# The place of the convolution of the recurrence's input among VectorE's work of the input projection

## What is computed

```python
h = rms_norm(x, in_norm_g[l])
proj = h @ w_in[l]                       # 1024 x 10240
q, k, v, g, xr, gr, m_ret, m_rnn = jnp.split(proj, SPLIT_POINTS, axis=-1)
q = rotary(q...); k = rotary(k...) * (RET_QK_DIM ** -0.5)
xr = causal_depthwise_conv(xr, lru_conv_w[l], lru_conv_b[l])     # 4 taps along the tokens
hr = rg_lru(xr, ...)
y_rnn = (hr * jax.nn.gelu(gr)) @ w_rnn_o[l]
...
```

## Time and profile before

| | |
|---|---|
| median of 3 runs | 2019.1 us (2016.65 to 2019.78) |
| profiled execution | 2018.14 us |
| its span | 2016.4 us |
| busy: PE, PEld, DVE, ACT, POOL | 1984.3, 1655.6, 1381.0, 907.0, 231.4 us |
| mean granted clock of TensorE | 0.999 |
| passes of the convolution (L1955, L1958) | 8 and 24; the first starts at 88.7, the last at 216.9 us |

### The profile page before, as it was taken

How to read it: one execution, slowest core, us unless ns; L and a number is a source line. 1 busy time by engine, 2 the same in 40 slices (tenths; PEclk the granted TensorE clock), 3 DMA queues, 4 the chain that set the end, 5 groups by cost and what they waited for, 6 DMA issues and landing times.

```text
span 2016.4 us, 25123 instructions
## 1 busy us (share of the span) xinstructions
PE 1984.3 (98%) x9304; PEld 1655.6 (82%) x9304; DVE 1381.0 (68%) x1661; ACT 907.0 (45%) x1155; POOL 231.4 (11%) x188
## 2 busy tenths in 40 slices
PE   8999999999999999999999999999999999999998
PEld 6788888888888888887888888998788888888887
DVE  6876776776744444614876776847988788776766
ACT  6443353343445555412544543345644545543335
POOL 0000010010000000001254554300000000000000
PEclk9999999999999999999999999999999999999999
DMA  6343444445444443445333244731222122156533
GB/s 255 115 155 116 166 161 173 166 157 177 171 166 174 157 157 125 146 151 188 100 121 122 77 124 142 264 132 63 85 83 104 63 83 104 62 181 231 204 102 132
DMA packets 185636, 285.10 MB, mean 141 GB/s; under 512 B 9824, under 2 KB 123872, under 8 KB 185312
## 3 DMA queue, kind: packets, MB, share of 16 engines
q1 hardware_dynamic: 165264, 206.62, 30.7%
q0 software_dynamic: 20304, 77.60, 9.9%
HBM read 200.29 MB, written 83.89 MB: 141 GB/s over the span
## 4 chain that ended last, share of the span: by engine, by line
PE 82%; DVE 11%; ACT 3%; issue 2%; DMA 1%; SPq 1%; DVEq 0%; ACTq 0%
PE ps L329 27%; PE ps L331 27%; PE ps L330 27%; DVE wx L2008 1%; DVE ws L312 1%; PE ps L1130 1%; DMA raw<-w_rnn_o 1%; DMA qkv<-scr_v 0%; DVE ost L1958 0%; DVE sc L2054 0%; DVE tt L1970 0%; ACT ri L1529 0%; DVE th L2194 0%; DVE ri L2205 0%; DVE th L2198 0%
## 5 line engine op out<-in xcount | busy, mean ns | idle before, releaser
L1384 ACT ACTIVATE wx<-raw 128x1024 fp32r<-128x1024 f32 (+1 forms) x152 | 137.3, 905 | 275.5 <-DVE raw L1984 151.5
L329 PE MATMUL ps<-xs,wx 128*128 128x512 f32 x612 | 239.0, 391 | 2.1 <-DVE xs L2430 1.6
L331 PE MATMUL ps<-xs,wx 128*128 128x512 f32 x612 | 238.2, 389 | 0.0
L330 PE MATMUL ps<-xs,wx 128*128 128x512 f32 x612 | 238.2, 389 | 0.0
L329 PE MATMUL ps<-sc,wx 128*128 128x512 f32 x448 | 175.6, 392 | 4.0 <-ACT ub L1419 3.9
L2008 DVE TENSOR_TENSOR wx<-raw,wx 128x1024 fp32r<-128x1024 f32 (+1 forms) x152 | 156.3, 1029 | 32.2 <-ACT wx L1384 32.2
L331 PE MATMUL ps<-sc,wx 128*128 128x512 f32 x448 | 175.0, 391 | 0.0
L330 PE MATMUL ps<-sc,wx 128*128 128x512 f32 x448 | 174.9, 390 | 0.0
L329 PEld LDWEIGHTS ps<-xs,wx 128*128 128x128 f32 x612 | 114.9, 188 | 28.4 <-issue 2.7
L331 PEld LDWEIGHTS ps<-xs,wx 128*128 128x128 f32 x612 | 114.9, 188 | 24.1
L330 PEld LDWEIGHTS ps<-xs,wx 128*128 128x128 f32 x612 | 114.9, 188 | 23.5
(11 more groups left out here) (282 smaller groups left out, 4803.9 us busy)
## 6 DMA issues: line engine op xcount, KB each, us to landing
raw<-w_in SPq DMA_DIRECT2D x80, 512.0 KB, 5.4
scr<-ost POOLq DMA_DIRECT2D x32, 1024.0 KB, 5.3
raw<-w_up SPq DMA_DIRECT2D x44, 512.0 KB, 3.9
tq<-w_down SPq DMA_DIRECT2D x88, 128.0 KB, 3.0
scr_t<-tq POOLq DMA_DIRECT2D x22, 512.0 KB, 3.2
scr_h<-vt POOLq DMA_DIRECT2D x11, 1024.0 KB, 4.3
scr_v<-ost POOLq DMA_DIRECT2D x8, 1024.0 KB, 4.7
qkv<-scr SPq DMA_DIRECT2D x64, 128.0 KB, 3.1
```

The lines of the kernel that those rows point to most:

```text
L329: pe.matmul(out, w(HI), x(HI), start=first, stop=False, skip_group_check=True)
L330: pe.matmul(out, w(HI), x(LO), start=False, stop=False, skip_group_check=True)
L331: return pe.matmul(out, w(LO), x(HI), start=False, stop=last, skip_group_check=True)
L1384: act.activation(dst, src, ACT.Copy).then_inc(sem["f_hi"], 1)
```

## The change

In the loop over b, for the blocks behind an xr block (b = 1, 3, 5, 7), the convolution half m = 0 moves from ahead of sum n = 0 to behind the low half of T4, and the half m = 1 from there to behind the sums n = 1 and 2.

```diff
--- before.py
+++ after.py
@@ -2126,8 +2126,6 @@
                     pair, slot = in_pair(b + 1)
                     combine_t13(b + 1, 1 - u, (raw_in[slot], pair * 32 + 32))
                     combine_t2(b + 1, 1 - u, 0)
-                if before == "xr":
-                    conv_rnn(b - 1, 0)
                 if before == "qk":
                     rotary(b - 1, 1)
                 in_c(b, u, 0)
@@ -2140,11 +2138,13 @@
                         dve.sem_inc(w_split[slot], IN_BLOCKS // 2)
                     split_lo(dve, V_PAIRS[0], 0)
                 if before == "xr":
-                    conv_rnn(b - 1, 1)
+                    conv_rnn(b - 1, 0)
                 if before == "qk":
                     rotary(b - 1, 0)
                 in_c(b, u, 1)
                 in_c(b, u, 2)
+                if before == "xr":
+                    conv_rnn(b - 1, 1)
                 if more:
                     prep_lo(b + 1, 1 - u, "t13", in_prepared(b + 1, "t13"))
                 in_c(b, u, 3)
```

## The result

The change takes 2021.56 us (median of 20 runs) against 2017.9 for the kernel before (median of 20): a ratio of 1.0018, interval 1.0012 to 1.0024, so +3.6 us (2.4 to 4.8). Forecast was +2.9. A ratio of 1 lies outside the interval, so the kernel is slower, though by less than the 0.2% that the prediction took for the limit of what a measurement can tell. Of each kernel one run lay far off, at 6226 and 2848 us; these two move the medians by at most 0.3 us and are left out of the ratio. The profiled executions have spans of 2016.4 and 2020.1 us, +3.7.

The account below looks back on a forecast made before the run. TensorE, busy 1984.3 of 2016.4 us, was taken as the bound, so only its waits or slower matmuls count. Gain -2.2, stall +3.4 and slow clock +1.7 gave +2.9 us, 2022.0 us; range 2016.9 to 2025.0.

Parts of the forecast that it names:

- The gain of 2.2 us in the odd blocks: Blocks 1, 3, 5, 7: earlier fourth weights let the U1 copy come on time, saving 0.35 + 0.61 + 0.64 + 0.62 us.
- The second half's place: VectorE: the second convolution half, behind sums n = 1 and 2, ends 17.42 us after A, PE's end of a block's second product.
- The P1 copy's margin: Blocks 2, 4, 6, 8: margin before PE's fourth product falls from 3.8 to about 0.2 us; no cost taken, at most 2.4.
- The store and the stall: Block 8: first sum waits for block 6's store, 9.04 us after the passes; PE's sixth product stalls 3.4 us, bounds 0 to 4.6.
- The slow clock: Behind block 8's stall: 3.5 us at the 1.2 GHz level, costing about 1.7 us, with 0 as the other end.
- The sum: Whole kernel: -2.2 + 3.4 + 1.7 = +2.9 us, giving 2022.0 us, chance 0.50.
- The store's quicker landing (1): Block 8: the store lands within 5.3 us, PE doesn't stall, only the 2.2 us gain is left: 2016.9 us; chance 0.12.
- the missing slow clock (2): Block 8: stall without the slow clock, +1.2 us, 2020.3 us; chance 0.12.
- The one by which the change is slower still (3): Block 8: block 10's load delays the store, stall 4.6, +4.1 us, 2023.2; with short P1 stalls 2025.6; chance 0.22.
- The queues: Block 8: if engines take turns between queues, block 6's store shares with block 10's load; the 4.6 us stall is likelier.

Follow-up runs that it names:

- Experiment 1: Against the kernel before: only the first convolution half moves behind T4's low half, the second following at once; 2015.44 us, ratio 0.9992.
- 5: The kernel before, VectorE's order unchanged, with ScalarE's U1 copy ahead of T4's high half in blocks 1, 3, 5 and 7; 2014.79 us, ratio 0.9986.
- experiment 4: The change, with the loads of cos and sin issued behind block 10's weight load; 2015.25 us, ratio 0.9992 to the kernel before.
- 7: The change, with cos and sin loaded behind block 10's weight load and block 0's P5 and U2 copies ahead of T4's high half; 2011.56 us, ratio 0.9968.
- 8: The change, with ScalarE's U1 copy ahead of T4's high half in block 8 alone; 2016.31 us, ratio 0.9994 to the kernel before.
- 9: The change, with block 0's P5 and U2 copies ahead of T4's high half, cos and sin loads left in place; 2015.84 us, ratio 0.9996.
- experiment 12: The changed kernel profiled once more with nothing altered, to look at the clock; span 2019.9 us against 2020.1.
- experiment 3: The change, but block 7 keeps the order of the kernel before; 2016.92 us, ratio 0.9999 to the kernel before.
- Experiment 2: Against the kernel before: only the second convolution half moves, behind the sums n = 1 and 2; 2022.06 us, ratio 1.0024.
- experiment 6: The kernel before, with ScalarE's P5 and U2 copies ahead of T4's high half in block 0 alone; 2017.52 us, ratio 0.9997.
- 11: The kernel before, with U1 copies ahead of T4's high half in blocks 1, 3, 5, 7 and block 0's P5 and U2 copies too; 2011.68 us, ratio 0.9973.
- 10: The kernel before, with only the loads of cos and sin moved behind block 10's weight load; 2018.03 us, ratio 1.0003.

## Why the prediction was right

- **The gain of 2.2 us in the odd blocks** was right in cause and nearly in size: the first three pairs give 0.34 + 0.55 + 0.61 where 0.35 + 0.61 + 0.64 were counted. Experiment 1 has all four pairs at 38.08, and 5 shows that the lateness acts through ScalarE's queue.
- **The second half's place** was computed as A + 17.42 and measured as A + 17.43.
- **The P1 copy's margin** of 0.2 held: no wait of PE in blocks 2, 4 and 6; in block 2 the copy ends at 110.04 and PE's fourth product starts at 110.28. The pairs take 38.09 to 38.15 us in the traces that have this order (the change, 4, 7, 8, 9, 12) wherever PE doesn't wait in block 8, against 38.08 in 1 and 5. That is 0.1 us in all, and how it comes about is not shown.
- **The store and the stall.** 9.04 from the end of the passes was taken, 9.09 measured; stall 3.4 forecast, 233.46 - 230.05 = 3.4 measured (the timeline's row gives 3.23 of idle time, since it reckons from the modelled end of the matmul before). Experiments 3 and 4 show the cause: without the move in block 7, or with cos and sin behind the store, the stall is gone. One detail was off: of the two loads only cos is issued ahead of the store, sin 0.05 us behind it (218.51 and 218.56 in the kernel before); the store still waits for both, as the packets below show.
- **The slow clock** came in the profile with the size forecast: the last pair is 43.23 long, 5.15 over the 38.08 without stalls, 3.4 of stall and 1.7 of clock. But a fixed 1.7 was the wrong form of this term. It differs by execution: 0, 1.4 to 1.8, or 2.8 to 2.9 (experiment 12). Behind block 8's stall the stretch came in all four traces that have it, with a price of 1.7 in the change, 2 and 9, and 2.9 in 12, so that it came near 1.7 there in the first profile is in part luck. The Trainium skill, TensorE: Matmul & The Clock Gate, section "Part 1: The HAM clock gate", says that the moment isn't tied to the kernel, and these traces agree; the sentence on that stood in the prediction, the sum took only one value.
- **The sum.** -2.2 + 3.4 + 1.7 = 2.9 against 3.0 measured in blocks 1 to 8, and 3.6 in the medians, whose interval reaches from 2.4 to 4.8. Of the 0.6 between nothing is shown: the draw of the clock behind either stall could be it, and so could the measurement, whose interval is wider. That the absolute times, 2022.0 and 2021.56, lie within 0.5 is luck too: the kernel before came out 1.2 lower with 20 runs than with the 3 of the prediction. Experiment 2, with the same stall, came out as forecast (1.0024 against 1.0025).
- **The rivals.** The store's quicker landing (1) and the missing slow clock (2) didn't come. The one by which the change is slower still (3) didn't come either: from issue to sum the store took 8.74 us instead of 8.68, and no short stalls came at the P1 copy.
- **The queues.** The packets that the traces record by queue show why block 10's load didn't hold the store up. In the changed kernel the first data packet of block 10's load starts at 227.89 and the last of the store at 228.92, so little was left to share. The Trainium skill, DMA: Bandwidth & Descriptors, section "Queues, rings and completion order", says that an engine takes turns between the queues that have work. For the store of block 6 and cos and sin these packets don't agree: cos and sin run from 221.53 to 226.29, and of the store's 256 packets the first starts at 225.97, only 18 of them ahead of the loads' last. In experiment 4, with those loads behind it, the store's first packet starts 1.27 us after the issue instead of 5.08. For block 7's store and block 10's load they do agree: both queues move data side by side from 228 us on. What makes the one case a queue and the other turns stays open.

## What to carry to other kernels

When an instruction is moved back on an engine that has no room, list what waits for its result and what stands behind it, and look for the one instance among many in which somebody is close: of the four places of the second half three were free, and the fourth, whose store others were waiting for, cost more than the first half's four gave. A stall that hides behind another one upstream shows only when that is gone, so an edit that does nothing alone (6) can be worth 4 us and more beside others: 7 is the change with its own stall removed (4, 0.9992) and this edit, and comes to 0.9968. Where an engine's queue carries a late operation ahead of a ready one that the bottleneck needs, putting the ready one first (5, 11) gives the same gain and moves nothing else.

## What the runs showed of the hardware that was not expected

The clock behind a stall is no constant of the program. Behind the same 3.0 us wait in block 0 it went to the 1.2 GHz level for 3.4 us in the kernel before, in the first profile of the change and in experiments 4, 5 and 10, for 6.8 us in experiment 3, and not at all in experiments 1, 2, 8 and 12. Experiment 1's trace, over the same stall:

```profile
76.00:84.00 8.00, 4.99 (x23) 4.13 (x23) 6.65 (x10) 3.61 (x5) 0.00 (x0) 1.00 0.21 75
```

and experiment 3's:

```profile
76.00:86.00 10.00, 7.00 (x19) 5.53 (x19) 6.19 (x9) 3.60 (x5) 0.00 (x0) 0.66 0.17 59
```

A wait of 2.65 us (experiment 6) brought it as well. A single pair of profiles can therefore differ by 1.4 to 2.9 us for each such stall without any cause in the code; the span of experiment 1 (2012.7) is 1.5 below that of experiment 4 (2014.2) at the same median, which is about one such stretch. It happens far from the change as well: near 930 us the clock is down for 3.4 us in the traces of 1, 3, 4, 5, 10 and 12 and stays up in the others. Experiment 1 first, then the kernel before:

```profile
920.00:940.00 20.00, 18.05 (x78) 14.26 (x78) 8.41 (x14) 2.23 (x5) 0.74 (x1) 0.91 0.66 228
```

```profile
920.00:940.00 20.00, 18.29 (x88) 14.85 (x87) 7.32 (x10) 3.90 (x6) 0.74 (x1) 1.00 0.46 155
```

The store was the other surprise: 1 MB issued between two loads of 0.5 MB each, 0.3 us behind the first and 0.05 ahead of the second, lands 8.7 us after its issue, against at most 4.5 with those loads behind it.
